# Cross attention's output projection from seven block products instead of eight, with three of four weight differences on GpSimd

## The chip, the core and the metric

The kernel runs on one core of a Trainium2 chip. The metric is the device time of one execution in microseconds, the median of several runs. The engines of the core work in parallel, each through its own queue in order: TensorE (PE in the profile, PEld its weight loads) multiplies matrices into PSUM, VectorE (DVE) and ScalarE (ACT) do elementwise work and reductions, GpSimd (POOL) does elementwise work on SBUF, and SyncE (SP) issues nearly all transfers from HBM. They wait for one another only by semaphores. All numbers are float32.

## The reference, cut to what matters

```python
for l in range(DEPTH):                       # 2 layers, SEQ = 256 rows, D_MODEL = 1024
    h = h + mixed @ w_out[l]                 # token mixers, left out here
    h = h + cross_attention(rms_norm(h, norm_cross[l]), rms_norm(mem, norm_mem[l]), ...)
    h = h + hier_moe(rms_norm(h, norm_ffn[l]), ...)
return rms_norm(h, final_norm)

def cross_attention(h, m, wq, wk, wv, wo):   # 4 heads of 256, 256 memory rows
    q, k, v = h @ wq, m @ wk, m @ wv
    p = softmax(q k^T * 256 ** -0.5)         # per head
    o = p v                                  # (256, 1024)
    return o @ wo                            # (256, 1024) x (1024, 1024)

def hier_moe(h, ...):                        # one of 4 groups, then 2 of its 8 experts
    for e in range(32):
        y += combine[:, e] * ((silu(t @ w_gate[e]) * (t @ w_up[e])) @ w_down[e])
```

Each layer reads 96 MB (in units of 2 MB: 48) of expert weights. The change is in `o @ wo` alone.

## The kernel before

The 256 rows are two row tiles of 128 (t = 0, 1), and the 1024 channels are eight chunks of 128 (c). A layer is one hand-written order of jobs. `LAYER_JOBS` names them with the PSUM bank that each fills (0 to 7) and the engine that empties it (V or A). A job may begin only when the job before it in its bank is emptied (`begin`). `pe_job` counts jobs that TensorE has finished, and `dve_emptied` and `act_emptied` count emptied banks. No scheduler reorders anything: the code's order on each engine is the order on the chip.

Weights come as units of at most 2 MB, in the order of `RING_ORDER`, into six ring slots (`ring0` to `ring5`). When TensorE has passed its last use of a slot it raises `unit_free` (`free_unit`), and SyncE, which goes through its list in order, issues the next load into it. Two slots are released in halves by `half_free`. In addition six buffers of the same size, `early0` to `early5`, lie over memory that the mixer and cross attention use. `early2` lies over `kT` and `vv`, `early3` over `mT` and `uT`, and `early4` over the residual `h` (its first half) and over `qT`, whose memory the attention outputs `oT` take as well. Each gets its expert unit once what it lies over is dead; `early4` gets it in quarters. This is the branch `if before == "xout0"` and its neighbours in `static_unit` (lines 517 to 531).

Cross attention ends as follows. The scores of row tile t come in two banks, `xs0` and `xs1` for t = 0, `xs2` and `xs3` for t = 1 (`scores`). VectorE takes negative maxima, ScalarE exponentials, VectorE divides by the sums (`probabilities`, L2177). TensorE transposes the probabilities (`turn_probabilities`, L1198), ScalarE copies them to `pT`. `outputs(t)` (L1208) makes o transposed, in the banks `xo0` to `xo3`, and `keep_outputs` copies them to `oT`. `to_rows` (L756) multiplies oT by the units `xout0` (output columns 0 to 511) and `xout1` (512 to 1023) of wo: four banks (t, n), each of eight matmuls of 128x128 by 128x512. VectorE adds each bank into `h` (`add_bank`, L1817). In the first layer it also scales the memory for the next layer in between (L2193, 128x2048). Behind the second scores TensorE's order is: outputs of tile 0, first bank of the projection, transposes of the probabilities of tile 1, start of the second bank, outputs of tile 1, and the rest.

Then `raw_transposes` turn the new rows of h for the router (`ffn_xt0` to `ffn_xt3`, L1258), `router` multiplies them (L1265), and VectorE chooses group and experts (`choose`, L2229 to L2246) before it adds the last bank `xout3` in two halves (`add_last_bank`, L2263). ScalarE forms the sums of squares, moves h into the PSUM sums (`start_sums`) and writes the normed rows `hn`. The gather by a 0/1 matrix (L794) and the experts (`up` L812, `down` L852) follow: eight quads of four experts, six units of 2 MB each. GpSimd works only in the set-up, on rotary angles.

The query projection of the same cross attention is already made of seven block products (`product`, L1176, with the differences `t1`, `s1` to `s4`). `query_blocks` gives the four blocks of its weights.

## Time and profile before

| | |
|---|---|
| median of 3 runs (lowest, highest) | 889.13 us (888.66, 893.29) |
| the profiled execution | 889.1 us |
| its span, first to last instruction | 887.3 us |
| PE busy in the span | 836.4 us |
| VectorE, ScalarE, GpSimd busy | 307.4, 166.2, 15.3 us |
| moved by DMA | 272.62 MB, mean 307 GB/s |
| mean granted clock of TensorE | 0.985 |

The profile is one execution. Its page gives busy times, the span in 40 slices, the chain of work that ended last, and groups of instructions by line. A timeline gives each instruction's start and length in us from the start of the span. A float32 matmul of L756 stands in the timeline as two records, so "x16" there are eight matmuls. A record's length includes the drain of the pipeline; what one costs is the distance of the starts. SyncE's rows (SPq) are moments of issue; the data lands later. A busy engine is not by itself a bound: what counts is who is waited for.

### The profile page before, as it was taken

The page shows a single profiled execution, that of the slowest core. Times are in us where ns is not written, and L with a number is a line of the kernel's source. Part 1 is how long each engine was busy: PE and PEld are TensorE (multiplying, and loading weights), DVE is VectorE, ACT ScalarE, POOL GpSimd, SP SyncE. Part 2 cuts the span into 40 slices and gives each one's busy share as a digit, 9 for nine tenths or more (in the row PEclk, how much of TensorE's full clock was granted, in tenths as well). Part 3 has the DMA queues.
Part 4 walks back from the last instruction along what each step waited for, and adds up shares of the span by engine and source line. Part 5 has one row for each costly group of instructions (what it writes and reads, how often), then busy time and mean ns, then how long its engine had stood idle before and what let it go on. Part 6 is the DMA issues. An engine that isn't in the chain of part 4 may idle for free.

```text
span 887.3 us, 12019 instructions
## 1 busy us (share of the span) xinstructions
PE 836.4 (94%) x5124; PEld 558.5 (63%) x5124; DVE 307.4 (35%) x601; ACT 166.2 (19%) x393; POOL 15.3 (2%) x21
## 2 busy tenths in 40 slices
PE   9999999999999999989879999999999999877876
PEld 8888886679665665545527888766975544332433
DVE  3327567355343111101104665744533421110102
ACT  1311135411131000000012112452122200000003
POOL 0600000000000000000000000000000000000000
PEclk9999999999999999999999999999999999888999
DMA  9953455076579999999999445507857899999995
GB/s 352 407 190 129 170 190 190 25 315 259 205 286 363 426 425 429 427 426 425 427 420 394 149 163 189 195 1 301 361 220 282 338 429 426 428 427 427 425 423 228
DMA packets 25943, 272.62 MB, mean 307 GB/s; under 512 B 3232, under 2 KB 3616, under 8 KB 7200
## 3 DMA queue, kind: packets, MB, share of 16 engines
q1 hardware_dynamic: 24592, 270.52, 74.8%
q10 hardware_dynamic: 1296, 1.30, 0.4%
q8 instruction: 43, 0.70, 0.3%
q14 instruction: 12, 0.10, 0.0%
HBM read 270.76 MB, written 1.05 MB: 306 GB/s over the span
## 4 chain that ended last, share of the span: by engine, by line
PE 73%; DMA 22%; SPq 2%; DVE 1%; issue 1%; ACT 0%; another core or an unknown queue 0%; PEld 0%; DVEq 0%; PEldq 0%; ACTq 0%
DMA early<-in_expert_units 19%; PE bank L674 17%; PE bank L756 12%; PE bank L812 7%; PE bank L1176 6%; PE bank L786 4%; PE bank L852 3%; PE bank L733 3%; PE bank L864 3%; DMA ring<-in_fixed_units 3%; PE bank L741 2%; PE bank L1189 2%; PE bank L996 2%; SPq L563 1%; PE bank L1208 1%; PE bank L695 1%
## 5 line engine op out<-in xcount | busy, mean ns | idle before, releaser
L674 PE MATMUL bank<-uT,ring 128*128 128x256 f32 x480 | 106.5, 381 | 0.0
L674 PEld LDWEIGHTS bank<-uT,ring 128*128 128x128 f32 x480 | 90.5, 190 | 13.2 <-DVE uT L1812 0.3
L812 PE MATMUL bank<-ring,xT 128*32 128x512 f32 x560 | 67.6, 621 | 12.0 <-DMA ring<-in_expert_units 11.8
L812 PE MATMUL bank<-early,xT 128*32 128x512 f32 x464 | 56.0, 620 | 13.1 <-DMA early<-in_expert_units 13.1
L786 PE MATMUL bank<-sel,hn 128*128 128x128 f32 x448 | 54.2, 280 | 3.0 <-issue 3.0
L756 PE MATMUL bank<-ring,early 128*128 128x512 f32 x128 | 56.7, 593 | 0.2 <-DVE early L2181 0.2
L2338 DVE TENSOR_TENSOR hid<-hid,bank 128x256 f32<-128x256 f32 x16 | 6.7, 421 | 142.1 <-ACT hid L1685 142.1
L756 PE MATMUL bank<-ring,uT 128*128 128x512 f32 x128 | 55.9, 592 | 0.0
L786 PEld LDWEIGHTS bank<-sel,hn 128*128 128x128 f32 x448 | 53.0, 197 | 3.7 <-issue 3.6
L864 PE MATMUL bank<-yy,states 128*128 128x512 f32 x112 | 54.4, 615 | 0.0
L812 PEld LDWEIGHTS bank<-ring,xT 128*32 128x32 f32 x560 | 17.4, 112 | 55.3 <-issue 39.7
L812 PEld LDWEIGHTS bank<-early,xT 128*32 128x32 f32 x464 | 14.2, 111 | 51.2 <-issue 37.5
L2343 DVE COPY yy<-bank 128x512 f32<-128x512 f32 x14 | 9.7, 692 | 100.3 <-PE bank L852 100.3
L1685 ACT ACTIVATE hid<-bank 128x256 f32<-128x256 f32 x16 | 6.1, 383 | 191.6 <-PE bank L812 191.6
L756 PEld LDWEIGHTS bank<-ring,uT 128*128 128x128 f32 x128 | 24.2, 190 | 27.9 <-issue 27.7
L756 PEld LDWEIGHTS bank<-ring,early 128*128 128x128 f32 x128 | 23.5, 190 | 26.2 <-issue 25.8
L864 PEld LDWEIGHTS bank<-yy,states 128*128 128x128 f32 x112 | 19.6, 193 | 29.4 <-issue 28.2
L2317 DVE TENSOR_TENSOR xT<-bank,ptab 128x512 f32<-128x512 f32 x28 | 19.3, 691 | 50.5 <-PE bank L786 50.5
L852 PE MATMUL bank<-ring,states 128*32 128x512 f32 x256 | 29.5, 596 | 1.7 <-DMA ring<-in_expert_units 1.7
L852 PE MATMUL bank<-early,states 128*32 128x512 f32 x192 | 22.2, 596 | 3.9 <-DMA early<-in_expert_units 3.9
L1817 DVE TENSOR_TENSOR early<-early,bank 128x512 f32<-128x512 f32 x14 | 9.6, 687 | 43.3 <-PE bank L756 43.3
L1176 PEld LDWEIGHTS bank<-uT,ring 128*128 128x128 f32 x192 | 22.2, 192 | 1.1 <-DVE uT L1812 0.5
(346 smaller groups left out, 1133.9 us busy)
## 6 DMA issues: line engine op xcount, KB each, us to landing
ring<-in_expert_units SPq DMA_DIRECT2D x47, 2048.0 KB, 22.0
early<-in_expert_units SPq DMA_DIRECT2D x37, 2048.0 KB, 25.6
ring<-in_fixed_units SPq DMA_DIRECT2D x16, 2048.0 KB, 8.5
ring<-in_fixed_units SPq DMA_DIRECT2D x24, 1024.0 KB, 18.9
early<-in_expert_units SPq DMA_DIRECT2D x12, 1024.0 KB, 38.0
ring<-in_expert_units SPq DMA_DIRECT2D x8, 1024.0 KB, 5.5
early<-in_expert_units SPq DMA_DIRECT2D x8, 512.0 KB, 5.3
ring<-in_fixed_units SPq DMA_DIRECT2D x4, 512.0 KB, 5.0
```

The source lines that it names most:

```text
L674: mm = pe.matmul(o[row0:row0 + m], w[:, c, c0:c0 + m], rhs[:, c], start=(c == 0), stop=(c == chunks - 1))
L733: mm = pe.matmul(o[:, t * S:(t + 1) * S], mem[:, c, t * P:t * P + P], w[:, c], start=(c == 0), stop=(c == KC - 1))
L741: mm = pe.matmul(o[:, t * S:(t + 1) * S], mem[:, c, t * P:t * P + P], w[:, c], start=(c == 0), stop=(c == KC - 1))
L756: mm = pe.matmul(o[:, :], rows, w[:, c], start=(c == 0), stop=(c == KC - 1))
L786: mm = pe.matmul(bank[half][:, c * P:c * P + P], hn[:, t, half * 4 + c], sel[:, t].rearrange("p e s -> p (e s)"), start=(t == 0), stop=(t ...
L812: mm = pe.matmul(bank[2][32 * e:32 * e + 32, :], xT[:, 2 * n + c, 32 * e:32 * e + 32], w[:, e, :, c], start=(n == 0 and c == 0), stop=(n = ...
L852: mm = pe.matmul(bank[n][32 * e:32 * e + 32, :], turned[:, 2 + c, 32 * e:32 * e + 32], w[:, e, c], start=(c == 0), stop=(c == 1), tile_pos ...
L864: mm = pe.matmul(sums(t, n)[:, :], turned[:, 4 * odd + t], yy[:, n * 512:n * 512 + 512], start=False, stop=False, skip_group_check=True)
L996: mm = pe.matmul(o[:, t * S:(t + 1) * S], uT[:, c, t * P:t * P + P], w[:, c], start=(c == 0), stop=(c == KC - 1))
L1176: mm = pe.matmul(o[:, k * P:(k + 1) * P], w[:, c, k * P:(k + 1) * P], rhs[:, c], start=(not onto and k == 0 and c == 0), stop=(c == KC // ...
L1189: mm = pe.matmul(o[:, k * S:(k + 1) * S], qT[:, t, 2 * hx + c], kT[:, 2 * hx + c], start=(c == 0), stop=(c == 1))
L2317: dve.tensor_tensor(xT[:, 4 * half:4 * half + 4], bank[half][:, :].rearrange("p (c s) -> p c s", c=4), gains[:, 3, 4 * half:4 * half + 4]. ...
```

## The change

The projection is taken as a 2 x 2 block product. The blocks of rows of o are the row tiles, its blocks of columns are chunks 0 to 3 and 4 to 7: o11, o12 (t = 0), o21, o22 (t = 1). The weight blocks are x11, x21 (upper and lower half of the rows of `xout1`) and x12, x22 (of `xout0`). Seven products of four matmuls are made instead of eight: `first_out` o11·x11, `xout1` o12·x21 on top of it in the same bank, `fifth_out` s1·T1, `sixth_out` s2·T2, `xout0` s3·x22 on top of the fifth, `xout2` s4·(x22 - x12) on top of the sixth, and `xout3` o22·(x21 - T2), with T1 = x12 - x11, T2 = x22 - T1, s1 = o21 + o22, s2 = s1 - o11, s3 = o12 - s2, s4 = o11 - o21. GpSimd makes T1 (into `kT`), T2 (over x11) and x22 - x12 (over x12), each 128x2048; it waits for `xs3`, the last reader of kT, and for `first_out`, the last reader of x11. VectorE makes x21 - T2 (128x2048, over x21) and s1 to s4 (128x512 each, into `pr`). It adds first_out's bank into three blocks of h, fifth_out's and sixth_out's into one each, xout2's into two (`add_product`), and the others into one (`add_bank`).

With this, TensorE transposes the probabilities of tile 1 directly behind the outputs of tile 0. SyncE's load into early2 waits for `fifth_out` (because of T1 in kT) and T2 instead of `xo3`, that into the third quarter of early4 for s4, and the slot of xout0 is released behind `xout2`. ScalarE's sums of squares of tile 0 take column half 1 first. The semaphore `fgate` becomes the first count of `diff`, which frees one semaphore for `out_blocks`.

```diff
@@ -265,8 +265,9 @@
-              ("xo0", "V", 5), ("xo1", "V", 6), ("xout0", "V", 1), ("xt2", "A", 2), ("xt3", "A", 3), ("xo2", "V", 4), ("xo3", "V", 5),
-              ("xout1", "V", 6), ("xout2", "V", 7), ("ffn_xt0", "V", 0), ("ffn_xt1", "V", 1), ("router0", "V", 3), ("ffn_xt2", "V", 0),
+              ("xo0", "V", 5), ("xo1", "V", 6), ("xt2", "A", 2), ("xt3", "A", 3), ("first_out", "V", 1), ("xo2", "V", 4), ("xo3", "V", 5),
+              ("xout1", "V", 1), ("fifth_out", "V", 7), ("ffn_xt1", "V", 1), ("sixth_out", "V", 0), ("xout0", "V", 7),
+              ("ffn_xt0", "V", 1), ("xout2", "V", 0), ("router0", "V", 3), ("ffn_xt2", "V", 0),
...
@@ -386,6 +387,8 @@
+        out_t1 = kT.rearrange("p c s -> p (c s)").rearrange("p (c n) -> p c n", c=KC // 2)
+        out_s = pr.rearrange("p t h s -> p (t h s)").rearrange("p (n c s) -> p n c s", n=4, c=KC // 2)
...
@@ -407,9 +410,9 @@
-        def query_blocks(lay):
-            left, right = (ring[RING_AT[lay, name] % RING][:, :].rearrange("p (c n) -> p c n", c=KC) for name in ("xq1", "xq0"))
+        def query_blocks(lay, names=("xq1", "xq0")):
+            left, right = (ring[RING_AT[lay, name] % RING][:, :].rearrange("p (c n) -> p c n", c=KC) for name in names)
             upper, lower = slice(0, KC // 2), slice(KC // 2, KC)
...
@@ -515,12 +518,13 @@
-                    sp.wait_ge(pe_job, INDEX[of, "xo3"] + 1)
+                    sp.wait_ge(pe_job, INDEX[of, "fifth_out"] + 1)
+                    sp.wait_ge(M["out_blocks"], in_layer(of, "out_blocks", 2))
-                    sp.wait_ge(pe_job, INDEX[of, "xout1"] + 1)
+                    sp.wait_ge(M["mixture"], in_layer(of, "mixture", 12))
-                    sp.wait_ge(pe_job, INDEX[of, "ffn_xt1"] + 1)
+                    sp.wait_ge(pe_job, INDEX[of, "ffn_xt0"] + 1)
...
@@ -752,10 +756,7 @@
-                    rows = oT[:, t, c] if prefix == "xout" else lhs[:, c, t * P:t * P + P]
-                    mm = pe.matmul(o[:, :], rows, w[:, c], start=(c == 0), stop=(c == KC - 1))
-                    if prefix == "xout" and t == T - 1 and n == 1 and c == KC // 2 - 1:
-                        mm.then_inc(half_free, 1)
+                    mm = pe.matmul(o[:, :], lhs[:, c, t * P:t * P + P], w[:, c], start=(c == 0), stop=(c == KC - 1))
...
@@ -1236,18 +1237,23 @@
+                for n in range(2):
+                    wait_unit(base, f"xout{n}")
-                after("xo0")
-                to_rows("xout", oT, base, 0, 0, range(4))
-                after("xo1")
-                to_rows("xout", oT, base, 0, 0, range(4, KC))
-                to_rows("xout", oT, base, 0, 1, range(2))
-                outputs(1)
-                to_rows("xout", oT, base, 0, 1, range(2, KC))
-                after("xo3")
-                to_rows("xout", oT, base, 1, 0)
+                x11, x12, x21, x22 = query_blocks(lay, ("xout1", "xout0"))
+                def row_product(o, rows, w, onto=False, chunks=range(KC // 2)):
+                    for c in chunks:
+                        mm = pe.matmul(o[:, :], rows[:, c], w[:, c], start=(not onto and c == 0), stop=(c == KC // 2 - 1), skip_group_check=True)
+                    return mm
+                def out_block(n):
+                    pe.wait_ge(M["out_blocks"], in_layer(lay, "out_blocks", n))
...
@@ -1287,16 +1293,40 @@
+                after("xo0")
+                row_product(begin("first_out"), oT[:, 0, 0:4], x11).then_inc(pe_job, 1)
+                outputs(1)
+                after("xo1")
+                row_product(begin("xout1"), oT[:, 0, 4:8], x21, onto=True).then_inc(pe_job, 1)
+                mixture(9)
+                out_block(1)
+                row_product(begin("fifth_out"), out_s[:, 0], out_t1).then_inc(pe_job, 1)
+                mixture(10)
+                out_block(2)
+                o = begin("sixth_out")
+                row_product(o, out_s[:, 1], x11, chunks=range(2))
+                raw_transposes(0, 1)
+                row_product(o, out_s[:, 1], x11, chunks=range(2, 4)).then_inc(pe_job, 1)
+                mixture(11)
+                row_product(begin("xout0"), out_s[:, 2], x22, onto=True).then_inc(pe_job, 1)
+                mixture(12)
+                out_block(3)
+                o = begin("xout2")
+                row_product(o, out_s[:, 3], x12, onto=True, chunks=range(2))
                 raw_transposes(0, 0)
-                raw_transposes(0, 1)
+                mixture(13)
+                pe.sem_inc(half_free, 1)
+                row_product(o, out_s[:, 3], x12, onto=True, chunks=range(2, 4)).then_inc(pe_job, 1)
+                o = begin("xout3")
+                row_product(o, oT[:, 1, 4:8], x21, chunks=range(2))
                 free_unit("xout2")
-                to_rows("xout", oT, base, 1, 1, range(3))
                 pe.wait_ge(M["params"], in_layer(lay, "params", 32))
+                last = o
                 o = begin("router0")
                 raw_transposes(1, 0)
-                to_rows("xout", oT, base, 1, 1, range(3, KC))
+                row_product(last, oT[:, 1, 4:8], x21, chunks=range(2, 4)).then_inc(pe_job, 1)
                 r1 = begin("router1")
...
@@ -1440,11 +1470,11 @@
-                for n in range(2):
+                for n in (1, 0) if ready == "xout" else (0, 1):
-                    act.activation(junk[:, half], src[:, t, half], ACT.Square, scale=D ** -0.5,
+                    act.activation(junk[n][:, :] if ready == "xout" else junk[:, half], src[:, t, half], ACT.Square, scale=D ** -0.5,
...
@@ -1659,12 +1689,12 @@
-                    act.wait_ge(dve_emptied, emptied(lay, ("xo2", "xo3", "xout1", "xout2")[2 * t + n]))
+                    act.wait_ge(dve_emptied, emptied(lay, ("xo2", "xo3", "xo1", "xout0")[2 * t + n]))
-                        sum_squares(h, hn[:, t].rearrange("p c k -> p (c k)"), t, "xout")
+                        sum_squares(h, (kept_p1, kept_u2), t, "xout")
...
@@ -2193,14 +2223,39 @@
                 probabilities(1)
+                def add_product(name, *to):
+                    o = job(name)
+                    for t, n in to:
+                        x = h[:, t, 512 * n:512 * n + 512]
+                        st(dve.tensor_tensor(x, x, o[:, :], ALU.add))
+                    settle()
+                    dve.sem_inc(dve_emptied, 1)
+                x11, x12, x21, x22 = query_blocks(lay, ("xout1", "xout0"))
+                o11, o12, o21, o22 = (oT[:, t, c] for t in range(T) for c in (slice(0, KC // 2), slice(KC // 2, KC)))
+                add_product("first_out", (0, 0), (1, 0), (1, 1))
+                keep_outputs(1)
+                dve.wait_ge(dve_emptied, emptied(lay, "xo3"))
+                mix(out_s[:, 0], o21, o22, ALU.add)
+                mixed(9)
+                mix(out_s[:, 1], out_s[:, 0], o11, ALU.subtract)
+                mixed(10)
+                mix(out_s[:, 2], o12, out_s[:, 1], ALU.subtract)
+                mix(out_s[:, 3], o11, o21, ALU.subtract)
+                add_bank("xout", 0, 1)
+                add_product("fifth_out", (1, 0))
+                keep_transposes("ffn", 3, 0, (1,))
+                dve.wait_ge(M["out_blocks"], in_layer(lay, "out_blocks", 2))
+                mix(x21, x21, x11, ALU.subtract)
+                add_product("sixth_out", (0, 0))
                 add_bank("xout", 0, 0)
-                keep_outputs(1)
-                add_bank("xout", 0, 1)
                 mean_square(4, 0)
+                keep_transposes("ffn", 3, 0, (0,))
                 refine(4, 0)
                 dve.sem_inc(M["ffn_rstd"], 1)
-                add_bank("xout", 1, 0)
-                keep_transposes("ffn", 3, 0)
+                add_product("xout2", (1, 0), (1, 1))
                 dve.wait_ge(M["params"], in_layer(lay, "params", 32))
...
@@ -2481,6 +2536,15 @@
+            for lay in range(L):
+                x11, x12, x21, x22 = query_blocks(lay, ("xout1", "xout0"))
+                pool.wait_ge(pe_job, INDEX[lay, "xs3"] + 1)
+                pool.tensor_tensor(out_t1, x12, x11, ALU.subtract).then_inc(M["out_blocks"], 1)
+                pool.wait_ge(pe_job, INDEX[lay, "first_out"] + 1)
+                pool.wait_ge(M["out_blocks"], in_layer(lay, "out_blocks", 1))
+                pool.tensor_tensor(x11, x22, out_t1, ALU.subtract).then_inc(M["out_blocks"], 1)
+                pool.tensor_tensor(x12, x22, x12, ALU.subtract).then_inc(M["out_blocks"], 1)
```

TensorE, first layer, from the outputs of tile 0 (`pT,vv`) on, before; `tab,pr` are the transposes of probabilities, `ring,early4` products of the projection, `tab,early4` the transposes of h:

```order
L1208 MATMUL bank5<-pT,vv 128x128 x8
L1208 MATMUL bank6<-pT,vv 128x128 x8
L756 MATMUL bank1<-ring3,early4 128x512 x8
L1198 MATMUL bank2<-tab,pr 128x128 x4
L1198 MATMUL bank3<-tab,pr 128x128 x4
L756 MATMUL bank6<-ring4,early4 128x512 x2
L1208 MATMUL bank4<-pT,vv 128x128 x8
L1208 MATMUL bank5<-pT,vv 128x128 x8
L756 MATMUL bank6<-ring4,early4 128x512 x6
L756 MATMUL bank7<-ring3,early4 128x512 x8
L1258 MATMUL bank0<-tab,early4 128x128 x4
```

The same place after; `kT,pr` is fifth_out, `ring,pr` the sixth, seventh and eighth on s2 to s4:

```order
L1209 MATMUL bank5<-pT,vv 128x128 x8
L1209 MATMUL bank6<-pT,vv 128x128 x8
L1199 MATMUL bank2<-tab,pr 128x128 x4
L1199 MATMUL bank3<-tab,pr 128x128 x4
L1251 MATMUL bank1<-ring4,early4 128x512 x4
L1209 MATMUL bank4<-pT,vv 128x128 x8
L1209 MATMUL bank5<-pT,vv 128x128 x8
L1251 MATMUL bank1<-ring4,early4 128x512 x4
L1251 MATMUL bank7<-kT,pr 128x512 x4
L1251 MATMUL bank0<-ring4,pr 128x512 x2
L1264 MATMUL bank1<-tab,early4 128x128 x4
L1251 MATMUL bank0<-ring4,pr 128x512 x2
```

The transposes of tile 1, which stood behind eight matmuls of the projection, stand directly behind the outputs of tile 0.

VectorE, first layer, from the scaling of the next layer's memory (`early5<-early5,ptab`) on, before; `pr<-pr,xsm` makes the probabilities of tile 1:

```order
L2193 TENSOR_TENSOR early5<-early5,ptab 128x2048
L2181 COPY early4<-bank5 128x512 [waits pe_job]
L2181 COPY early4<-bank6 128x512 [waits pe_job]
L2175 RECIPROCAL xsm<-xsm 128x4 [waits x_exp]
L2177 TENSOR_TENSOR pr<-pr,xsm 128x1024 [waits dve_step]
L1817 TENSOR_TENSOR early4<-early4,bank1 128x512 [waits pe_job]
L2181 COPY early4<-bank4 128x512 [waits pe_job]
L2181 COPY early4<-bank5 128x512 [waits pe_job]
L1817 TENSOR_TENSOR early4<-early4,bank6 128x512 [waits pe_job]
```

The same place after; `early4<-early4,bank` adds a product into h, `pr<-` with `early4` makes s1 to s4:

```order
L2223 TENSOR_TENSOR early5<-early5,ptab 128x2048
L2211 COPY early4<-bank5 128x512 [waits pe_job]
L2211 COPY early4<-bank6 128x512 [waits pe_job]
L2205 RECIPROCAL xsm<-xsm 128x4 [waits x_exp]
L2207 TENSOR_TENSOR pr<-pr,xsm 128x1024 [waits dve_step]
L2232 TENSOR_TENSOR early4<-early4,bank1 128x512 [waits pe_job]
L2232 TENSOR_TENSOR early4<-early4,bank1 128x512 x2
L2211 COPY early4<-bank4 128x512 [waits dve_step,pe_job]
L2211 COPY early4<-bank5 128x512 [waits pe_job]
L2174 TENSOR_TENSOR pr<-early4 128x512 [waits dve_emptied]
L2174 TENSOR_TENSOR pr<-pr,early4 128x512 [waits mixture]
L2174 TENSOR_TENSOR pr<-early4,pr 128x512 [waits mixture]
```

The order up to the probabilities of tile 1 is the same; behind it come three additions for the first product, and the four sums of 128x512.

GpSimd, behind the set-up, the first layer's three instructions, which are new; ring4 is xout1's slot, ring3 xout0's:

```order
L2542 TENSOR_TENSOR kT<-ring3,ring4 128x2048 [waits pe_job]
L2545 TENSOR_TENSOR ring4<-ring3,kT 128x2048 [waits out_blocks,pe_job]
L2546 TENSOR_TENSOR ring3<-ring3 128x2048
```

SyncE's list keeps its order. Its rows around the changed waits, before:

```order
L500 DMA early2<-in_expert_units 128x4096 [waits pe_job]
L506 DMA early4<-in_expert_units 128x1024 [waits pe_job]
L553 DMA ring3<-in_expert_units 128x4096 [waits unit_free]
L506 DMA early4<-in_expert_units 128x1024 [waits h_moved,normed,pe_job]
L535 DMA ring4<-in_expert_units 128x2048 [waits half_free]
```

and after:

```order
L503 DMA early2<-in_expert_units 128x4096 [waits out_blocks,pe_job]
L509 DMA early4<-in_expert_units 128x1024 [waits mixture]
L557 DMA ring3<-in_expert_units 128x4096 [waits unit_free]
L509 DMA early4<-in_expert_units 128x1024 [waits h_moved,normed,pe_job]
L539 DMA ring4<-in_expert_units 128x2048 [waits half_free]
```

The kinds of waits of the first two are other ones; the third, ring3, waits for a count that TensorE raises later in its order.

## Rows read from the trace of the kernel before

**Rows 1.** The page, the chain that ended last, shares of the span by engine.

```profile
PE 73%; DMA 22%; SPq 2%; DVE 1%; issue 1%; ACT 0%; another core or an unknown queue 0%; PEld 0%; DVEq 0%; PEldq 0%; ACTq 0%
```

**Rows 2.** Windows: us, busy us of each engine, PEclk, DMA share, GB/s.

```profile
268.00:271.00 3.00, 2.59 (x24) 1.39 (x24) 1.19 (x5) 1.59 (x3) 0.00 (x0) 1.00 0.46 164
...
275.00:470.00 195.00, 180.97 (x1280) 100.44 (x1276) 25.00 (x51) 18.54 (x35) 0.00 (x0) 1.00 1.01 426
...
700.00:865.00 165.00, 140.91 (x1004) 62.71 (x1000) 23.45 (x46) 11.04 (x21) 0.00 (x0) 0.93 1.01 426
```

**Rows 3.** Timeline of SyncE's queue: start us, length us, what is issued.

```profile
240.19 0.33 SPq L500 DMA_DIRECT2D early<-in_expert_units  x1
...
252.31 0.33 SPq L553 DMA_DIRECT2D ring<-in_expert_units  x1
...
270.67 0.33 SPq L535 DMA_DIRECT2D ring<-in_expert_units  x1
...
694.91 0.33 SPq L535 DMA_DIRECT2D ring<-in_expert_units  x1
```

**Rows 4.** Timeline of TensorE, first layer: start us, length us, what, idle before.

```profile
226.87 7.13 PE L756 MATMUL bank<-ring,early 128*128 128x512 f32 x16 [0.21 <-DVE early L2181]
...
236.43 3.73 PE L1208 MATMUL bank<-pT,vv 128*128 128x128 f32 x32
...
240.00 12.18 PE L756 MATMUL bank<-ring,early 128*128 128x512 f32 x28
...
252.02 1.04 PE L1258 MATMUL bank<-tab,early 128*128 128x128 f32 x8
...
252.89 2.74 PE L756 MATMUL bank<-ring,early 128*128 128x512 f32 x6
...
255.47 1.87 PE L1265 MATMUL bank<-w_rout,pT 128*128 128x36 f32 x16
```

**Rows 5.** Timeline of TensorE, second layer, the same places.

```profile
651.14 7.03 PE L756 MATMUL bank<-ring,early 128*128 128x512 f32 x16
...
679.64 1.87 PE L1265 MATMUL bank<-w_rout,pT 128*128 128x36 f32 x16
```

**Rows 6.** Timeline of VectorE, first layer, from the last score bank on.

```profile
223.12 0.69 DVE L2169 TENSOR_REDUCE xsm<-bank 128x2 f32<-128x512 f32 x1 [0.83 <-PE bank L1189]
...
223.93 2.28 DVE L2193 TENSOR_TENSOR early<-early,ptab 128x2048 f32<-128x2048 f32 x1
...
226.13 1.28 DVE L2181 COPY early<-bank 128x512 f32<-128x512 f32 x2
...
227.53 1.22 DVE L2177 TENSOR_TENSOR pr<-pr,xsm 128x1024 f32<-128x1024 f32 x1
```

**Rows 7.** Timeline of VectorE, second layer, normalisation of the second probabilities.

```profile
652.15 1.23 DVE L2177 TENSOR_TENSOR pr<-pr,xsm 128x1024 f32<-128x1024 f32 x1
```

**Rows 8.** Timeline of VectorE, first layer, router and last output bank.

```profile
260.38 0.15 DVE L2280 TENSOR_SCALAR minus_half<-ss 128x1 f32<-128x1 f32 x1
...
262.14 0.75 DVE L2263 TENSOR_TENSOR early<-early,bank 128x256 f32<-128x256 f32 x2 [1.62 <-PE bank L756]
```

**Rows 9.** Timeline of VectorE, second layer, end of that chain.

```profile
684.55 0.15 DVE L2280 TENSOR_SCALAR minus_half<-ss 128x1 f32<-128x1 f32 x1
...
686.32 0.75 DVE L2263 TENSOR_TENSOR early<-early,bank 128x256 f32<-128x256 f32 x2 [1.62 <-PE bank L756]
```

**Rows 10.** Timeline of VectorE and GpSimd in the set-up, side by side.

```profile
21.68 2.29 DVE L1888 TENSOR_TENSOR early<-early,mV 128x2048 f32<-128x2048 f32 x1
...
21.81 2.95 POOL L2488 TENSOR_SCALAR mkT<-mkT,tab 128x256 f32<-128x256 f32 x1
...
25.44 1.13 POOL L2491 TENSOR_SCALAR mkT<-mkT 128x256 f32<-128x256 f32 x1
...
25.90 0.43 DVE L1890 CAST lvmask<-hg 128x512 uint8<-128x512 f32 x1 [1.93 <-DMA hg<-in_level_masks]
...
30.37 0.72 POOL L2496 TENSOR_TENSOR mkT<-mkT 128x256 f32<-128x256 f32 x1
```

10 lines of the change are left out of this document (5 added, 5 removed).

## The prediction

> **What bounds the kernel now.** I read the chain that ended last first. TensorE has 73% of it and DMA 22% [rows 1]: most of the time goes as TensorE goes, but there are stretches in which only transfers count. The windows show which. From 275 to 470 us and from 700 to 865 us, the expert stages of the two layers, the DMA share is 1.01 at 426 GB/s; these stretches last as long as their bytes take, whatever TensorE does in them. In the window 268 to 271 just ahead it is 0.46 [rows 2]. So in each layer TensorE's pace up to the moment when the queue becomes full decides, and behind it the bytes do. That moment is the issue into the first half of ring5, at 270.67 in the first layer and 694.91 in the second [rows 3]. It is released by the first expert matmuls, which follow the router. The question for each edit is therefore by how much it moves the router's last results, and whether the transfers ahead of that issue are still done in time.
>
> **TensorE, what goes.** The 28 records from 240.00 to 252.02 are 0.429 us apart [rows 4]. A matmul is two records, 0.859 us, and a block product of four is 3.43 us. One of eight goes in each layer: 3.43 us a layer, 6.87 us in all. That is the most that the change can give.
>
> **TensorE, what the new order costs.** The transposes of the second tile's probabilities need `pr` normalised. Before, eight matmuls of the projection stood ahead of them, from 226.87 on, so the normalisation was long done. Now they stand directly behind the outputs of tile 0. VectorE's order up to there is unchanged: in the first layer the scaling of the memory (2.28 us from 223.93), two copies of output banks (from 226.13), and the normalisation from 227.53 for 1.22 us, done at 228.75 [rows 6]. TensorE restarts some 0.05 us behind that, at 228.80 against 226.87 [rows 4]: 1.93 us of wait. In the second layer there is no scaling, but the copy of the second output bank needs that bank, so the normalisation runs from 652.15 for 1.23 us and ends at 653.38 [rows 7]; TensorE restarts at 653.43 against 651.14 [rows 5]: 2.29 us. Queued behind these transposes on TensorE is everything else.
>
> From the restart to the router TensorE has: 8 transposes 0.87 (252.02 to 252.89), first product 3.43, outputs of tile 1 3.57 (236.43 to 240.00), five products 17.17, eight transposes in two parts 0.87 and half a product 1.72 [rows 4]: 27.6 us. The router's first matmul is then at 256.40 (before 255.47 [rows 4]) and 681.03 (before 679.64 [rows 5]): later by 0.93 and 1.39 us: of the four matmuls saved only one stood ahead of the router. Behind it there are now two matmuls of the last product, 1.72 us, instead of five, 4.29.
>
> Are the operands there in time? I followed the first layer through. first_out is ready at 233.3; VectorE adds it three times at 0.64 each (two copies take 1.28 [rows 6]), done 235.4; the outputs of tile 1 are copied by 237.7, s1 is done at 238.4, s2 at 239.1, s3 and s4 by 240.5. TensorE asks for s1 at 240.1 and for s2 at 243.5. VectorE then adds the second bank (241.2) and the fifth (244.5), copies a transposed bank, makes x21 - T2 (2.28, as the scaling; done 249.0) and adds the sixth (249.7). TensorE asks for that bank at 250.8. No wait, with 1 us to spare at the narrowest place. In the second layer the distances are the same.
>
> **GpSimd, three differences a layer.** The trace has no 128x2048 on GpSimd. Its nearest is the 128x256 tensor-tensor, 0.72 us [rows 10]. Scaled by 8 it is 5.8 us; with a fixed part of 0.16 us (an estimate; VectorE's 0.64 and 2.28 us for 512 and 2048 elements [rows 6] give 0.1) it is 4.6. I take 4.6 to 5.8 and reckon with 4.6 because VectorE's rows show such a fixed part. T1 then runs from 223.2 (VectorE sees the last score bank at 223.12 [rows 6]), T2 from 233.4 to 238.0, x22 - x12 to 242.6. They are wanted at 240.1, 243.5 and 250.8. At 5.8 each, and with all VectorE work on two SBUF operands in the way of them (2.6 us for s1 to s4, 2.28 for x21 - T2), the second ends near 241.8 and the third near 250: still in time. So their own length costs nothing; with 1 us more it would begin to.
>
> **Do the two engines hinder each other?** In the set-up VectorE's product on two SBUF operands runs 21.68 to 23.97 at its usual 2.29. GpSimd's instruction begun at 21.81 takes 2.95, where others there take 0.7 to 1.1; it ends 0.8 behind VectorE's. The one at 25.44 takes 1.13; VectorE's cast begun inside it at 25.90 takes 0.43 and is not held up [rows 10]. Here GpSimd gives way and VectorE doesn't. I take that: no cost to VectorE. The other bound, VectorE held for a whole GpSimd instruction, is the second case below. The Trainium skill, "SBUF — State Buffer", section "Who interferes with whom", says that VectorE with two SBUF inputs and a GpSimd instruction that reads SBUF exclude each other, and that whoever starts first holds the shared ports for the whole instruction. By that rule VectorE would wait here, and the time would be that of case 2; the trace agrees for the instruction at 21.81 and does not show it for the cast at 25.90, though all its GpSimd instructions are short.
>
> **What is late next.** From the router on VectorE has the chain logits, transposed bank, choice of group and experts. It begins with the router's result and ends at 260.38 + 0.15 = 260.53, that is 5.06 us behind the router's first matmul at 255.47; in the second layer 684.70 - 679.64 = 5.06 as well [rows 4, 5, 8, 9]. Before, it had to wait then: it added the last bank only at 262.14 and 686.32, when TensorE had made it [rows 8, 9]. Now that bank is ready 4.1 us behind the router's first matmul (router 1.72, transposes 0.43, two matmuls 1.72, their drain 0.2), so VectorE's chain ends last. It reaches the last bank at 256.40 + 5.06 = 261.46 and 681.03 + 5.06 = 686.09. That is 0.68 and 0.23 us earlier than before. Of 3.43 us a layer, 1.93 and 2.29 go into the wait for the probabilities, and 0.82 and 0.91 into this chain.
>
> **DMA.** Load by load, first layer: early2 goes out when the fifth product is done, at 243.7 instead of 240.19. ring3 went out at 252.31, 0.58 us ahead of the end of the transposes behind which its release stands (252.89) [rows 3, 4]; now the release stands behind the first half of the last product (256.40), so at 255.8. From there to the first half of ring5 there are 5.5 MB in order, at 4.92 us per 2 MB (426 GB/s [rows 2]) 13.5 us: done 269.3 plus the time from issue to first data. The issue into ring5 comes at 270.67 - 0.68 = 269.99 plus the same. So the queue is drained 0.7 us ahead of it, and nothing is lost; with gaps between the loads up to 1 us may be. The second layer has the same distances. ScalarE's new order of squares lies ahead of the bank it waits for; I cost it at nothing.
>
> **Sum.** 0.68 + 0.23 = 0.9 us against the profiled execution's 889.1 (span 887.3 plus 1.8 around it), which is the median of 889.13 to within 0.03: 888.2 us.
>
> **Case 1, the sum (chance 0.54).** 888.2; its own range 886.5 to 891.0: above by the DMA margins, and by 1 us a layer if GpSimd slows VectorE a little; below if the chain behind the router runs tighter.
>
> **Case 2, slower: VectorE is held by GpSimd's instructions (0.36).** T1 starts at 223.2, 0.7 us ahead of the scaling of the memory, which has two SBUF operands. Held to 227.8, the scaling ends at 230.1 instead of 226.2, and the probabilities come 3.9 us later (5.1 at 5.8). In the second layer only the normalisation is held, 0.4 us. The second place is s1: it is ready to run at 241.5 when T2 runs to 241.9 and x22 - x12 right behind it to 246.5. If the latter gets in first, the fifth product waits 3.3 us; if s1 gets between, s2 is held and TensorE waits 0.5. Sum: 4.3 + 2 x 0.5 to 2 x 3.3, less 0.9: 893.5 to 899.1, with the longer instructions 901. For it: the GpSimd instruction starts first and is several times as long as any of the set-up, so the cast at 25.90 may have met one that had already read its operands. Against it: that cast, the only one begun inside a GpSimd instruction that has a length to judge by [rows 10]. From a hold of 0.9 us in all the change is no gain, from 5.3 us it is slower by more than 0.5%.
>
> **Case 3, part of it or another small wait (0.07).** GpSimd is stretched past 6 us by VectorE's work and T2 or x22 - x12 comes late: 1 to 2 us in each layer, 890 to 892.
>
> **Case 4, the whole product is gained (0.03).** If the waits for the probabilities and for the choice did not bind, 889.1 - 6.87 = 882.2. Against it stand rows 6 to 9, which give those times directly.
>
> **How the numbers follow.** A change of this kernel's time can be told from none at about 0.5%, 4.4 us. Cases 1 and 3 lie within it, and a seventh of case 2 with it: 0.54 + 0.07 + 0.05, less 0.02 of case 1's tails, is 0.64. Slower by more is the rest of case 2 and a tail: 0.32. Faster is case 4 and a tail, 0.04. The range goes from 886.5 to 898, which leaves out case 4, the top of case 2 and tails.
>
> **What would show it.** Right: TensorE idle 1.9 and 2.3 us ahead of the transposes of tile 1 (now L1199) for `pr`; GpSimd 4.6 to 5.8 us each; the scaling of the memory at 2.28 us; VectorE adding the last bank without a wait for TensorE; ring5's first half issued 0.2 to 0.7 us earlier; expert stages at 426 GB/s of unchanged length. Wrong: the scaling at 6 us or starting late (case 2), TensorE waiting for s1, s2, T2 or x22 - x12, idle DMA between 257 and 271, or a gain at the router above 2 us.

## The result: 1.2% slower, where no change was forecast

Changed: 899.95 us median of 4 runs (898.54 to 901.27). Before, on the same chip: 889.50 (888.66 to 893.29). Ratio 1.0118, 95% interval 1.0103 to 1.0133. Forecast was 888.2, range 886.5 to 898. The profiled execution took 900.04 with a span of 898.2, 10.9 more than before.

The chain of waits of the changed kernel looks like before's [rows 1]; the one share that has grown clearly is VectorE's, from 1 to 3%:

```profile
PE 70%; DMA 21%; DVE 3%; SPq 2%; issue 2%; PEld 1%; ACT 0%; another core or an unknown queue 0%; DVEq 0%; PEldq 0%; ACTq 0%
```

The timelines say where. GpSimd (start us, length us, what, idle before), T1, T2 and x22 - x12 of the first layer and T1 of the second, then VectorE, first layer, from the last score bank on, and the same place in the second:

```profile
223.12 4.50 POOL L2542 TENSOR_TENSOR kT<-ring 128x2048 f32<-128x2048 f32 x1 [185.50 <-PE bank L1190]
239.46 4.53 POOL L2545 TENSOR_TENSOR ring<-ring,kT 128x2048 f32<-128x2048 f32 x1 [11.84 <-PE bank L1251]
243.94 4.96 POOL L2546 TENSOR_TENSOR ring<-ring 128x2048 f32<-128x2048 f32 x1
...
653.46 4.51 POOL L2542 TENSOR_TENSOR kT<-ring 128x2048 f32<-128x2048 f32 x1 [404.55 <-PE bank L1190]
```

```profile
223.79 3.85 DVE L2201 TENSOR_SCALAR xsm<-xsm 128x2 f32<-128x2 f32 x1
227.56 2.28 DVE L2223 TENSOR_TENSOR early<-early,ptab 128x2048 f32<-128x2048 f32 x1
229.76 1.27 DVE L2211 COPY early<-bank 128x512 f32<-128x512 f32 x2
...
231.16 1.23 DVE L2207 TENSOR_TENSOR pr<-pr,xsm 128x1024 f32<-128x1024 f32 x1
239.41 1.88 DVE L2232 TENSOR_TENSOR early<-early,bank 128x512 f32<-128x512 f32 x3 [7.03 <-PE bank L1251]
...
244.58 4.88 DVE L2174 TENSOR_TENSOR pr<-pr,early 128x512 f32<-128x512 f32 x1
...
654.14 3.86 DVE L2201 TENSOR_SCALAR xsm<-xsm 128x2 f32<-128x2 f32 x1
657.91 1.28 DVE L2211 COPY early<-bank 128x512 f32<-128x512 f32 x2
```

The row to look at is VectorE's first. A tensor-scalar on two elements per partition takes 3.85 us, and ends at 227.64, when GpSimd's T1 (223.12 + 4.50 = 227.62) ends. No semaphore stands between the two: the engines do wait for one another otherwise than the opening section says. Everything behind it on VectorE keeps its length and comes 3.6 us late against [rows 6], the probabilities at 232.39. The second layer has the same hold at the same small instruction. A third is s2, 4.88 us: it ends at 249.46, 0.56 behind the end of x22 - x12 (243.94 + 4.96 = 248.90). That one costs TensorE nothing here, since the sixth product comes directly behind the fifth, at 249.66. Not held are the three additions from a PSUM bank at 239.41, though T2 runs beside them at its usual 4.53.

TensorE, the same places as [rows 4, 5]:

```profile
232.44 1.97 PE L1199 MATMUL bank<-tab,pr 128*128 128x128 f32 x8 [5.83 <-DVE pr L2207]
234.20 5.18 PE L1251 MATMUL bank<-ring,early 128*128 128x512 f32 x8
239.22 3.73 PE L1209 MATMUL bank<-pT,vv 128*128 128x128 f32 x32
...
262.74 1.87 PE L1271 MATMUL bank<-w_rout,pT 128*128 128x36 f32 x16
...
660.59 1.96 PE L1199 MATMUL bank<-tab,pr 128*128 128x128 f32 x8 [3.64 <-DVE pr L2207]
662.34 4.45 PE L1251 MATMUL bank<-ring,early 128*128 128x512 f32 x8
```

The idle is 5.83 and 3.64 us where 1.93 and 2.29 were forecast. And what runs behind it is slow: transposes 1.97 instead of 1.04, first product 5.18 instead of 3.6. The windows (us, busy of each engine, granted clock, DMA share, GB/s) give the reason; the clock stood at 0.50, 1.2 GHz, behind the idle, and behind the router of the second layer once more:

```profile
229.00:232.40 3.40, 0.00 (x0) 0.00 (x0) 3.35 (x5) 0.00 (x0) 0.00 (x0) 0.73 0.47 202
...
234.20:236.00 1.80, 1.80 (x4) 0.77 (x4) 0.00 (x0) 0.60 (x1) 0.00 (x0) 0.50 0.00 0
...
237.50:239.20 1.70, 1.70 (x5) 0.76 (x4) 0.00 (x0) 0.00 (x0) 0.00 (x0) 1.00 0.00 0
281.00:476.00 195.00, 182.62 (x1280) 100.93 (x1276) 24.62 (x49) 18.92 (x36) 0.00 (x0) 0.99 1.01 426
...
698.50:700.00 1.50, 1.50 (x9) 1.50 (x9) 1.29 (x9) 0.68 (x1) 0.00 (x0) 0.50 1.02 431
```

The expert stages run at 426 GB/s as before [rows 2], so the loss is all ahead of them. SyncE's issues into the first half of ring5, against 270.67 and 694.91 [rows 3]:

```profile
276.24 0.33 SPq L539 DMA_DIRECT2D ring<-in_expert_units  x1
...
705.21 0.33 SPq L539 DMA_DIRECT2D ring<-in_expert_units  x1
```

They are 5.57 and 10.30 us later. In the first layer the router's first matmul comes at 262.74, 6.34 later than the forecast 256.40: 3.64 from the hold (232.44 against 228.80), 2.48 from the clock (232.44 to 239.22 is 6.78 instead of 0.87 + 3.43), 0.2 the rest. In the second layer the hold costs 1.52 (the copies there wait for TensorE anyway), the clock 1.73 at the transposes and the first product (660.59 to 666.62) and about 1.5 behind the router, where the gather's 16 matmuls take 3.38 instead of 2.01.

### The profile page after: what moved, and what is told of

The parts are those of the page before. It is cut to its first block, busy times and chain, and to the rows that moved or that the text cites. A ratio compares the mean times of both kernels' runs of the same rounds, so it can differ in the third digit from the quotient of the medians.

```text
span 898.2 us, 12037 instructions
## 1 busy us (share of the span) xinstructions
PE 836.5 (93%) x5108; PEld 557.9 (62%) x5108; DVE 340.6 (38%) x623; ACT 166.8 (19%) x393; POOL 43.1 (5%) x27
## 2 busy tenths in 40 slices
DMA packets 25943, 272.62 MB, mean 304 GB/s; under 512 B 3232, under 2 KB 3616, under 8 KB 7200
## 4 chain that ended last, share of the span: by engine, by line
PE 70%; DMA 21%; DVE 3%; SPq 2%; issue 2%; PEld 1%; ACT 0%; another core or an unknown queue 0%; DVEq 0%; PEldq 0%; ACTq 0%
DMA early<-in_expert_units 19%; PE bank L678 16%; PE bank L813 7%; PE bank L759 6%; PE bank L1177 6%; PE bank L1251 5%; PE bank L787 3%; PE bank L737 3%; PE bank L853 3%; DMA ring<-in_fixed_units 2%; PE bank L865 2%; PE bank L745 2%; PE bank L1190 2%; PE bank L997 2%; SPq L567 1%
## 5 line engine op out<-in xcount | busy, mean ns | idle before, releaser
L813 PE MATMUL bank<-early,xT 128*32 128x512 f32 x464 | 58.0, 638 | 16.7 <-DMA early<-in_expert_units 16.7
L2542 POOL TENSOR_TENSOR kT<-ring 128x2048 f32<-128x2048 f32 x2 | 9.0, 4508 | 590.0 <-PE bank L1190 590.0
L1251 PE MATMUL bank<-ring,early 128*128 128x512 f32 x48 | 24.3, 647 | 0.0
L1177 PE MATMUL bank<-uT,ring 128*128 128x128 f32 x192 | 22.4, 275 | 0.0
```

Of the source, the lines that this page charges most:

```text
L813: mm = pe.matmul(bank[2][32 * e:32 * e + 32, :], xT[:, 2 * n + c, 32 * e:32 * e + 32], w[:, e, :, c], start=(n == 0 and c == 0), stop=(n = ...
L1177: mm = pe.matmul(o[:, k * P:(k + 1) * P], w[:, c, k * P:(k + 1) * P], rhs[:, c], start=(not onto and k == 0 and c == 0), stop=(c == KC // ...
L1251: mm = pe.matmul(o[:, :], rows[:, c], w[:, c], start=(not onto and c == 0), stop=(c == KC // 2 - 1), skip_group_check=True)
```

## Experiments

Theory H: a VectorE instruction that has only SBUF operands and a GpSimd instruction exclude each other; whoever has begun keeps the other out until its end. Rival R: only bandwidth is shared and VectorE merely goes slower. Theory C: the idle that the hold makes lowers TensorE's clock, and that is a part of the price of its own. Each kernel was timed beside the kernel before on the same chip.

**1. T1 started behind the probabilities.**

```diff
                 pool.wait_ge(pe_job, INDEX[lay, "xs3"] + 1)
+                pool.wait_ge(M["x_p"], in_layer(lay, "x_p", 2))
```

> The changed kernel, with GpSimd's first difference begun only when the probabilities of tile 1 are written. Theory H (a GpSimd instruction of 4.5 us that reads SBUF holds back every VectorE instruction that needs the second port until it ends, and the longer wait lets TensorE's clock fall to 0.5): the small scaling of the maxima is back at 0.17 us instead of 3.85, the probabilities end near 228.8 and 2.3 us behind the outputs in the second layer, TensorE waits 1.9 and 2.3 us, its clock stays at 1.00, and the time is 888 to 890 us. Rival R (any wait at this place drops the clock, and the order of the transposes is the cause): the clock falls here too, 892 to 894 us. Rival S (the hold does not come from overlap with GpSimd): 900 us as before.

892.34 against 889.18, ratio 1.0033 (1.0012 to 1.0053). VectorE, GpSimd and TensorE, first layer:

```profile
223.93 0.17 DVE L2201 TENSOR_SCALAR xsm<-xsm 128x2 f32<-128x2 f32 x1
...
238.78 4.88 DVE L2174 TENSOR_TENSOR pr<-pr,early 128x512 f32<-128x512 f32 x1
```

```profile
228.98 4.52 POOL L2543 TENSOR_TENSOR kT<-ring 128x2048 f32<-128x2048 f32 x1 [191.86 <-DVE pr L2207]
...
238.14 4.97 POOL L2547 TENSOR_TENSOR ring<-ring 128x2048 f32<-128x2048 f32 x1
```

```profile
228.89 1.10 PE L1199 MATMUL bank<-tab,pr 128*128 128x128 f32 x8 [2.15 <-DVE pr L2207]
229.82 3.60 PE L1251 MATMUL bank<-ring,early 128*128 128x512 f32 x8
...
262.47 0.68 PE L1282 MATMUL bank<-tab,early 128*128 128x128 f32 x4 [0.66 <-DVE early L2318]
```

One wait takes away 7.6 us. The hold of the small scaling is gone, TensorE's idle is 2.15 us, near the forecast, and the clock stays up there. s2 is still held, until 243.66, but the sixth product's turn comes only at 243.71. In the first layer ring5's first half goes out at 271.93, where 269.99 was forecast: 0.54 us of that is there at the router already (256.94 against 256.40), 1.4 is the gather behind it, 3.42 us at a clock of 0.50 from 266 to 268. In the second layer the clock is 0.50 from 692 to 694.

**2. The hold left in, TensorE kept busy through the idle.**

```diff
                 outputs(0)
+                keep_busy(2, 20)
                 turn_probabilities(1)
```

> The changed kernel, with 20 matmuls of 128x128 that nothing reads put on TensorE into the wait ahead of the transposes of tile 1. Nothing on VectorE or GpSimd is moved. Theory H: the hold of VectorE stays (3.85 us in both layers), but the granted clock stays at 1.00, so the eight transposes take 0.87 us and the first product 3.43; 2.5 and 1.7 us come back, and 1.5 more of the second fall in the second layer if that hangs on the first: 894 to 896 us. Rival (the slow transposes and product come from something else, as GpSimd reading the same weights): no change, 900 us.

897.52 against 889.18, ratio 1.0097 (1.0074 to 1.0119): 2.4 us better than the changed kernel by the medians, though the intervals of the two ratios overlap, and 4.0 by the spans (894.2; the profiled execution was the fastest of four). VectorE's scaling is still held (3.87 and 3.85 us), but the clock is 1.00 in the window 229 to 233, and TensorE runs the transposes in 1.09 and the product in 3.60 us:

```profile
231.69 1.09 PE L1199 MATMUL bank<-tab,pr 128*128 128x128 f32 x8 [1.39 <-DVE pr L2208]
232.62 3.60 PE L1252 MATMUL bank<-ring,early 128*128 128x512 f32 x8
```

So C holds there. The rows give the size better than the times: from the transposes to the outputs of tile 1 it is 4.36 and 4.31 us instead of 6.78 and 6.03, 4.1 us less in all, and in the second layer the added matmuls outlast the wait and give some 0.7 of it back. The clock's share comes on top of the hold. It fell once more behind the second router (0.50 from 696 to 698, gather 3.01 us), so that fall does not hang on the ones before the transposes.

**3. Each GpSimd instruction as four of 128x512.**

```diff
+                    for c in range(KC // 2):
+                        i = pool.tensor_tensor(out[:, c], x[:, c], y[:, c], ALU.subtract)
...
-                pool.tensor_tensor(out_t1, x12, x11, ALU.subtract).then_inc(M["out_blocks"], 1)
+                in_parts(out_t1, x12, x11)
...
```

> The changed kernel, with each of GpSimd's three instructions of 128x2048 issued as four of 128x512. Theory H (the port is kept for the length of one instruction): VectorE gets in between two of them, so the scaling of the maxima takes at most 1.4 us instead of 3.85 and the second sum s2 at most 1.4 instead of 4.88; TensorE's wait shrinks to 3 to 4 us; 890 to 895 us. Rival (VectorE gets in only when GpSimd's queue is empty): 3.85 us or more as before, 900 us or above.

894.61 against 889.18, ratio 1.0057 (1.0038 to 1.0076). VectorE and GpSimd, first layer, from an execution that was the slowest of six (897.88):

```profile
223.86 0.61 DVE L2201 TENSOR_SCALAR xsm<-xsm 128x2 f32<-128x2 f32 x1
224.38 2.28 DVE L2223 TENSOR_TENSOR early<-early,ptab 128x2048 f32<-128x2048 f32 x1
...
227.98 2.11 DVE L2207 TENSOR_TENSOR pr<-pr,xsm 128x1024 f32<-128x1024 f32 x1
```

```profile
223.18 8.03 POOL L2544 TENSOR_TENSOR kT<-ring 128x512 f32<-128x512 f32 x4 [185.94 <-PE bank L1190]
```

The hold ends with the first quarter: 0.61 us instead of 3.85. Then it is GpSimd's turn to wait: its four quarters take 8.03 us, which is the 4.5 of one piece and VectorE's two instructions of 2.28 and 1.22 us. A lock held for an instruction, as H says; shared bandwidth would not depend on how the work is cut. The clock fell all the same, to 0.50 in both layers (first layer: transposes 1.97 us), behind idles of 3.48 and 2.60 us.

**4. The kernel before, with only the transposes of tile 1 moved forward.**

```diff
...
                 outputs(0)
+                turn_probabilities(1)
                 after("xo0")
...
-                turn_probabilities(1)
                 to_rows("xout", oT, base, 0, 1, range(2))
```

> The kernel before, with nothing changed but that the transposes of tile 1's probabilities stand directly behind the outputs of tile 0, as in the changed kernel; no GpSimd work, eight products. The prediction's term: TensorE waits 1.9 and 2.3 us more and nothing else moves, so 889.5 + 4.2 = 893.7 us, with the clock at 1.00. If a wait of 2 us is enough to drop the clock, another 1.7 to 2.5 us a layer: 897 to 898 us. If other slack hides the wait: under 892 us.

894.29 against 889.18, ratio 1.0057 (1.0037 to 1.0076). TensorE waits 2.15 and 2.13 us for the probabilities; router, last bank and ring5's issue are all 1.95 us later in the first layer (272.62 against 270.67). In the second layer the router is 2.35 us later, counted from the transposes of tile 0's probabilities (646.47 to 685.29 against 643.17 to 679.64). The clock stays at 1.00 at these places. That term of the forecast (1.93 and 2.29) has its size, and the new order of TensorE alone is a loss. A further 1.35 us were lost in the profiled execution between the two places; why stays open.

**5. The kernel before, with T1 added, result unused.**

```diff
+                pe.wait_ge(M["out_blocks"], in_layer(lay, "out_blocks", 1))
                 to_rows("xout", oT, base, 0, 1, range(2))
...
+            for lay in range(L):
+                x11, x12, x21, x22 = query_blocks(lay, ("xout1", "xout0"))
+                pool.wait_ge(pe_job, INDEX[lay, "xs3"] + 1)
+                pool.tensor_tensor(out_t1, x12, x11, ALU.subtract).then_inc(M["out_blocks"], 1)
```

> The kernel before, eight products as it has them, with one thing more: GpSimd's first difference, started where the changed kernel starts it, its result used by nobody (TensorE waits for it only behind the transposes of tile 1, where it has long been done). It prices that one instruction. Theory H (VectorE's 2-element scaling waits for all of it): the scaling takes 3.9 us in both layers, the copies of tile 0's outputs behind it come 3.6 us late in layer 0 and about 2.9 in layer 1, TensorE waits for them with nothing else to do, and the clock may fall after it: 6.5 to 10 us more, 896 to 900. Rival (the loss in the changed kernel came from its missing cover before the transposes, and with eight products it is hidden): 889.5, within 0.3%.

896.54 against 888.82, ratio 1.0085 (1.0070 to 1.0101). One GpSimd instruction of 4.51 us a layer, of which nobody uses the result:

```profile
223.94 3.85 DVE L2175 TENSOR_SCALAR xsm<-xsm 128x2 f32<-128x2 f32 x1
```

```profile
230.64 8.83 PE L757 MATMUL bank<-ring,early 128*128 128x512 f32 x16 [3.90 <-DVE early L2185]
...
658.48 7.13 PE L757 MATMUL bank<-ring,early 128*128 128x512 f32 x16 [1.70 <-DVE early L2185]
```

TensorE waits 3.90 and 1.70 us for the copies behind the held scaling, and in the first layer the clock (0.50 from 231 to 234) adds 1.7 more. The loss needs neither seven products nor the new order.

**6. T1 behind the maxima, so that the small scaling goes first.**

```diff
                 pool.wait_ge(pe_job, INDEX[lay, "xs3"] + 1)
+                pool.wait_ge(M["x_max"], in_layer(lay, "x_max", 4))
```

> The changed kernel with GpSimd's first difference started a fraction of a microsecond later, behind the maxima of tile 1, so that the 2-element scaling can run ahead of it. Theory H (any VectorE instruction with both operands in SBUF waits for the whole of GpSimd's 4.5 us): the 2-element scaling takes 0.17 again, and in layer 0 the 128x2048 scaling behind it is held instead, from 224.0 to about 228.5, so that the probabilities come 4.5 us later than without GpSimd; in layer 1, where copies from PSUM stand there, these are not held and the normalisation is, to about 655.5, 2 us later than without. With the clock falling behind the longer idle: 896 to 900. Rival: only the 2-element form is held, for a reason of its own (its operand as a scalar): nothing is held, and the time is that of the first difference behind the probabilities, 892.3. Rival: only the port is shared and VectorE goes slower beside GpSimd: the 128x2048 scaling takes 2.8 to 3.4 us instead of 2.28, 893 to 894.5.

897.24 against 889.68, ratio 1.0074 (1.0053 to 1.0095). The time is as expected, one step of the reason was not:

```profile
223.84 2.28 DVE L2223 TENSOR_TENSOR early<-early,ptab 128x2048 f32<-128x2048 f32 x1
226.04 1.28 DVE L2211 COPY early<-bank 128x512 f32<-128x512 f32 x2
227.24 0.17 DVE L2205 RECIPROCAL xsm<-xsm 128x4 f32<-128x4 f32 x1
227.44 4.12 DVE L2207 TENSOR_TENSOR pr<-pr,xsm 128x1024 f32<-128x1024 f32 x1
```

```profile
224.09 6.39 POOL L2543 TENSOR_TENSOR kT<-ring 128x2048 f32<-128x2048 f32 x1 [186.12 <-DVE xsm L2201]
```

VectorE's scaling began 0.25 us ahead of T1, so it was T1 that waited: 6.39 us, its 4.5 behind the scaling's end at 226.0. Then the normalisation is held until T1 ends at 230.5 (4.12 us instead of 1.22). In between, the copies from PSUM run at full speed, and so does the reciprocal on four SBUF elements, 0.17 us. Who began first has the way, in both directions, and not every SBUF instruction of VectorE needs it. The clock fell in both layers, behind idles of 5.05 and 3.15 us.

**7. All four differences on VectorE, none on GpSimd.**

```diff
...
+                dve.tensor_tensor(out_t1, x12, x11, ALU.subtract).then_inc(M["out_blocks"], 1)
                 add_product("first_out", (0, 0), (1, 0), (1, 1))
...
+                dve.tensor_tensor(x11, x22, out_t1, ALU.subtract).then_inc(M["out_blocks"], 1)
...
                 add_product("fifth_out", (1, 0))
+                dve.tensor_tensor(x12, x22, x12, ALU.subtract).then_inc(M["out_blocks"], 1)
...
-                pool.tensor_tensor(out_t1, x12, x11, ALU.subtract).then_inc(M["out_blocks"], 1)
...
```

> The changed kernel with the three differences of GpSimd computed by VectorE: the first behind the probabilities of tile 1, the second behind the sums of the first product, the third behind the sum of the fifth. Theory H (VectorE loses its time because an instruction with both operands in SBUF waits for the whole of a GpSimd instruction): nothing is held, the 2-element scaling is back at 0.17 us, and the second mixture at 0.69 where it was 4.88. The three differences take 2.3 us each on VectorE, which is idle for 4.6 us at the first place and can give the second and third (each before its product needs it), so the time is that of the kernel whose first difference waits for the probabilities (892.3 measured) or up to 1 us under it: 891 to 893. Rival R (the change asks too much of VectorE, GpSimd or not): the copies and mixtures behind the second difference come 2.3 us late and TensorE waits for them in both layers: 895 to 898.

890.03 against 889.68, ratio 1.0005 (0.9992 to 1.0018). Each difference takes 2.28 us there, half of GpSimd's 4.5, and nothing waits for it. Ring5's issue in the first layer:

```profile
270.02 0.33 SPq L539 DMA_DIRECT2D ring<-in_expert_units  x1
```

The forecast had 269.99. So with the work off GpSimd the first layer goes as forecast, and the whole is no different from before. In the second layer the clock fell behind a wait of 2.12 us (0.59 from 654 to 658) and took 1.7 us; in the first it stayed at 1.00 behind a wait of 2.15.

**8. Experiment 1 with 12 matmuls where TensorE waits behind the router.**

```diff
                         if half == 0:
+                            for _ in range(12):
+                                pe.matmul(o[:, 0:P], ident, tb("before"), start=True, stop=True)
```

> The kernel whose first difference waits for the probabilities, with 12 matmuls of 128x128 into an unused bank where TensorE waits 0.66 us for the last sum behind the router. In that kernel the granted clock was 0.50 at 266 to 268 and 692 to 694, with the gather's 16 matmuls at 3.42 us instead of 2.01. Theory C (that second fall of the clock comes from the idle behind the router, which the longer VectorE chain makes): the clock stays at 1.00, the first load behind the router is issued 1.2 to 1.8 us earlier in each layer, and the time is 889 to 890 (892.3 without). Rival: the matmuls themselves stand in the way, or the clock falls anyway: 892 to 893.5.

894.65 against 889.68, ratio 1.0052 (1.0031 to 1.0073): a miss, 2.3 us above experiment 1 by the medians. In the profiled execution the clock stayed at 1.00 behind the router in both layers, and the gather took 2.01 us. By itself that shows little: experiments 6 and 7 have the same wait of 0.66 us without the matmuls, and their gather takes 2.01 us too. All traces together say more. In the seven kernels with this wait and nothing in it, the gather is slow (2.76 to 3.50 us) in 7 of 14 layers; in the others it takes 2.01 us in all 12. The wait goes with the fall, but does not settle it. The matmuls took 2.92 us in a gap of 0.66, and from the small scaling to ring5's issue it is 48.29 us with them (271.17 - 222.88) and 48.00 without (271.93 - 223.93). They cost about what a fall costs. The profiled execution, 892.0, was the fastest of five; why the others took up to 3.8 us more stays open.

**9. Three of the first product's four matmuls ahead of the transposes.**

```diff
+                row_product(o, oT[:, 0, 0:4], x11, chunks=range(3))
+                turn_probabilities(1)
+                row_product(o, oT[:, 0, 0:4], x11, chunks=range(3, 4)).then_inc(pe_job, 1)
```

(on top of experiment 1)

> Of the kernel that took 885.65 only the first two edits: the first difference behind the probabilities, and three of the first product's four matmul pairs ahead of the transposes of tile 1. The third difference and the product around the router are where the changed kernel has them. Against the kernel with the first difference alone moved (892.3) it saves the 2.15 us wait in each layer: 887.5 to 888.5. The rest, to 885.65, would then be the router's place and the clock behind it. Rival (the router's place does nothing, the wait was all of it): 885.5 to 886.5.

893.18 against 888.82, ratio 1.0043 (1.0029 to 1.0057): a miss of 5 us. The wait is gone, and the time is not. TensorE, then VectorE:

```profile
229.81 1.04 PE L1199 MATMUL bank<-tab,pr 128*128 128x128 f32 x8
...
243.87 1.98 PE L1250 MATMUL bank<-ring,pr 128*128 128x512 f32 x4 [1.21 <-DVE pr L2176]
```

```profile
236.19 2.72 DVE L2176 TENSOR_TENSOR pr<-early 128x512 f32<-128x512 f32 x1
238.94 4.88 DVE L2176 TENSOR_TENSOR pr<-pr,early 128x512 f32<-128x512 f32 x1
```

The sixth product starts at 243.87; in experiment 1 it starts at 243.71. It waits for s2, and s2 for x22 - x12: three GpSimd instructions in a row, from the probabilities on, end at 243.27 here and at 243.11 there. What was a just hidden hold is now the bound. The gather is slow here too (3.27 and 2.76 us), as in experiment 1.

**10. Experiment 9, with x22 - x12 behind s4 and the whole last product behind the router's of tile 0.**

```diff
+                pool.wait_ge(M["mixture"], in_layer(lay, "mixture", 12))
                 pool.tensor_tensor(x12, x22, x12, ALU.subtract).then_inc(M["out_blocks"], 1)
...
-                row_product(o, oT[:, 1, 4:8], x21, chunks=range(2))
...
-                row_product(last, oT[:, 1, 4:8], x21, chunks=range(2, 4)).then_inc(pe_job, 1)
+                row_product(last, oT[:, 1, 4:8], x21).then_inc(pe_job, 1)
```

> A kernel with the mechanism answered: the first difference behind the probabilities, three of the four matmuls of the first product ahead of the transposes of tile 1 (they need no probabilities of it), the third difference behind the last mixture of the outputs, and the whole last product behind the router's of tile 0, so that VectorE's 5 us of choosing lie beside TensorE's work. Theory H with C: the 2.15 us of waiting for the probabilities go in each layer (less what three matmuls of 0.43 us x 2 leave over), the second mixture is held no more, and the 0.66 us wait and the second fall of the clock behind the router go: 4 x 2 us off the 892.3, 883 to 886. Rival (the wait for VectorE only moves to another place): 888 to 891.

885.65 against 889.68, ratio 0.9944 (0.9926 to 0.9962). TensorE, first layer:

```profile
256.43 3.60 PE L1250 MATMUL bank<-ring,early 128*128 128x512 f32 x8
...
260.68 0.64 PE L1281 MATMUL bank<-tab,early 128*128 128x128 f32 x4
...
263.35 2.01 PE L795 MATMUL bank<-sel,hn 128*128 128x128 f32 x16
```

Four matmuls now cover VectorE's choosing, the 0.66 us wait is gone, and the clock stays up (gather 2.01 us). Of the holds only s1's is left, 2.73 us under T2, and in the second layer TensorE waits 0.56 us for it. Ring5's issue is at 268.61, 3.5 us ahead of experiment 9. The two edits were not run apart, so how much each gives stays open.

**11. The same with all differences on VectorE.** The order of experiment 10 on TensorE, the differences as in experiment 7.

> The kernel that took 885.65 with all four differences on VectorE and none on GpSimd. Theory H: in that kernel the first mixture is still held (2.73 and 3.17 us instead of 0.69) and TensorE waits 0.1 and 0.6 us for it; without GpSimd nothing is held, but the differences take 2.3 us each of VectorE in front of copies and mixtures: 884.5 to 886. Rival (VectorE has not the time): 887 to 889.

884.15 against 888.82, ratio 0.9947 (0.9933 to 0.9960), ring5 at 268.10. That is 0.35 us under the expected range. By the ratio it is level with experiment 10; both are faster than the kernel before and the changed one.

## Why the prediction was wrong

- **The step that failed** is in "Do the two engines hinder each other?": "Here GpSimd gives way and VectorE doesn't. I take that: no cost to VectorE." The row for it was the cast at 25.90 [rows 10], 0.43 us inside a GpSimd instruction. Experiments 1, 3, 5 and 6 show the exclusion. The instruction at 21.81 had shown it, in the direction in which VectorE had begun first. The cast is no counter-proof: the reciprocal of experiment 6 shows that some VectorE instructions on SBUF are not held. What sets the cast and the reciprocal apart was not tried. The rule that the prediction cited against itself (the Trainium skill, "SBUF — State Buffer", "Who interferes with whom") says in its own words "Whoever issues first gets the shared pair for the whole instruction", and the traces of 3 and 6 agree. But the part that the prediction took from it speaks of two SBUF inputs, and the instruction held first has one and a constant.
- **Case 2 happened, with its terms off.** It let the 128x2048 scaling be the first one held, since it has two SBUF operands, and so priced the second layer, where copies from PSUM stand there, at 0.4 us. The one that was held is the tensor-scalar on two elements ahead of it, in both layers: 3.64 and 1.52 us. The second place of case 2 cost nothing: s1 got between T2 and x22 - x12, s2 was held, and TensorE did not wait for it.
- **The clock was no term at all.** At 2 us of idle I reckoned TensorE unchanged. Behind 5.83 and 3.64 us it fell and took 2.48 and 1.73 more, and 1.5 behind the second router. With the hold alone the sum would be 888.2 + 3.64 + 1.52 = 893.4, inside the range and next to case 2's lowest value, 893.5. The clock's 5.7 make it 899.1, of 899.95 measured; the rest is not accounted for. That this equals the top of case 2 is chance: case 2 got there by a wait for s1 that did not happen.
- **Right:** the wait for the probabilities without hold (1.93 and 2.29; experiments 1 and 4: idle 2.15, in 4 a delay of 1.95 and 2.35), the choosing behind the router (5.06; measured 267.72 - 262.74 = 4.98, the last bank added without a wait for TensorE), GpSimd's 4.6 us (4.50), the expert stages. With no GpSimd in the way the first layer of experiment 7 follows these terms to 0.03 us, and the second lost 1.7 to the clock; in the times, 890.03 against 889.68, the forecast gain of 0.9 is not found.
- **Where the saved 3.43 us a layer went:** 2 into the wait for the probabilities, 1 into the choosing, and the rest, 0.65 in the first layer of experiment 7 (270.02 against 270.67), is too little for the times to show; the hold and the clock are the loss on top. Experiments 10 and 11, which give TensorE other work at both places, get 4 to 5 us of the 6.87 back.

## What to carry to other kernels

Work put on GpSimd isn't free because GpSimd is idle: look at what VectorE issues in the 4.5 us behind its start, down to the smallest instruction, and start it where VectorE works from PSUM or not at all, or cut it in parts. Price a wait of TensorE with the clock that may fall behind it. And when a wait is filled, ask what was hidden behind it: here the filled 2.15 us gave nothing until the second hold was moved too.
